# Decay logits of a gated linear attention from one rounded product with 98 rows, and eight dense products per tile at another place

## What is computed

```python
h = rmsnorm(x, norm_g)
proj = h @ w_in       # q, k, v of three branches, low-rank decay features glr, z paths, gates
gate_logits = einsum('btir,irk->btik', glr, w2) + b2      # glr: 2 directions x rank 16; k: 4 heads x 64
log_a = log_sigmoid(gate_logits) / 16                     # the decays of both directions
o_a = gla_branch(q, k, v, log_a) * silu(z_a)              # chunked scan, forward and backward
o_b = diff_attention(...) * silu(z_b)
o_c = memory_cross_attention(...) * silu(z_c)
x = x + (sum_i sigmoid(gate_i) * (o_i @ w_branch[i])) @ w_out
return rmsnorm(x, final_norm_g)
```

## Time and profile before

| what | before |
|---|---|
| median of three runs | 3404.91 us (3400.65 to 3405.81) |
| the profiled execution, its own time | 3406.49 us |
| its span, first to last instruction | 3404.7 us |
| TensorE busy | 3281.1 us, 96% of the span |
| VectorE busy | 1989.6 us, 58% |
| ScalarE busy | 1324.1 us, 39% |
| GpSimd busy | 1106.1 us, 32% |
| granted TensorE clock, mean | 0.985 |

### The profile page before, as it was taken

The page is one execution under the profiler, slowest core; times in us unless marked ns, Lnnn a source line. Parts: engine busy times, 40 slices in busy tenths (PEclk is TensorE's granted clock), DMA queues, the critical chain, the costliest instruction groups (busy, mean ns, idle before and its releaser), DMA issues. The chain is left out here.

```text
span 3404.7 us, 50932 instructions
## 1 busy us (share of the span) xinstructions
PE 3281.1 (96%) x19032; PEld 2557.6 (75%) x19032; DVE 1989.6 (58%) x4609; ACT 1324.1 (39%) x2165; POOL 1106.1 (32%) x511
## 2 busy tenths in 40 slices
PE   7999999998999999999999988999999888999998
PEld 6888888886878888888877765666666556888887
DVE  3322312226566656665568788888888566556654
ACT  3111111114334343344323336767676555333322
POOL 3322323243333343333333325555555433000000
PEclk9999999999999999999999999999999999999999
DMA  6545445565454544544448965122221266667562
GB/s 214 182 153 188 154 156 176 173 208 177 133 182 146 180 151 125 190 145 141 131 161 292 324 210 155 45 75 64 67 62 38 100 229 229 226 230 237 176 217 75
DMA packets 317906, 554.89 MB, mean 163 GB/s; under 512 B 35421, under 2 KB 114525, under 8 KB 317662
## 3 DMA queue, kind: packets, MB, share of 16 engines
q1 hardware_dynamic: 266510, 471.26, 42.9%
q10 hardware_dynamic: 51152, 80.38, 6.5%
HBM read 382.03 MB, written 169.50 MB: 162 GB/s over the span
## 5 line engine op out<-in xcount | busy, mean ns | idle before, releaser
L731 POOL TENSOR_TENSOR glaf_w_lo<-early_raw,glaf_w_hi 128x1024 fp32r<-128x1024 f32 x140 | 350.0, 2500 | 638.6 <-ACT glaf_w_hi L705 638.6
L760 PE MATMUL glaf_dense_acc<-h_hi,glaf_w_hi 128*128 128x512 f32 x1120 | 444.0, 396 | 4.1 <-ACT glaf_dense_out L714 4.1
L760 PE MATMUL glaf_dense_acc<-h_lo,glaf_w_hi 128*128 128x512 f32 x1120 | 446.6, 399 | 0.0
L760 PE MATMUL glaf_dense_acc<-h_hi,glaf_w_lo 128*128 128x512 f32 x1120 | 437.0, 391 | 0.0
L1749 DVE CUSTOM_DVE_ANT_0 front_p<-diff_s_ps,ahead_table 128x512 f32<-128x512 f32 x544 | 347.4, 687 | 74.0 <-PE diff_s_ps L1611 73.0
L514 POOL TENSOR_TENSOR proj_w_lo<-early_raw,proj_w_hi 128x1024 fp32r<-128x1024 f32 x84 | 204.6, 2438 | 478.9 <-DVE proj_w_hi L476 478.9
L1692 ACT ACTIVATE front_p<-front_p,diff_neg_max 128x2048 f32<-128x2048 f32 (+1 forms) x160 | 278.7, 1743 | 7.0 <-DVE diff_neg_max L1757 7.0
L1635 PE MATMUL diff_oT_ps<-diff_aT,diff_v 128*128 128x512 f32 x544 | 273.3, 603 | 5.2 <-ACT diff_aT L1686 5.2
L201 PE MATMUL proj_acc<-h_hi,proj_w_hi 128*128 128x512 f32 x672 | 262.8, 391 | 0.0
L203 PE MATMUL proj_acc<-h_hi,proj_w_lo 128*128 128x512 f32 x672 | 261.6, 389 | 0.0
L202 PE MATMUL proj_acc<-h_lo,proj_w_hi 128*128 128x512 f32 x672 | 261.5, 389 | 0.0
(11 more groups left out here) (215 smaller groups left out, 7149.1 us busy)
## 6 DMA issues: line engine op xcount, KB each, us to landing
early_raw<-in_w_zg SPq DMA_DIRECT2D x180, 512.0 KB, 4.7
early_raw<-in_w_stream SPq DMA_DIRECT2D x80, 512.0 KB, 3.6
scratch_zg<-glaf_dense_out SPq DMA_DIRECT2D x140, 256.0 KB, 2.3
items_raw<-in_w_br SPq DMA_DIRECT2D x120, 256.0 KB, 2.9
merge_gate<-scratch_zg SPq DMA_DIRECT2D x120, 256.0 KB, 3.2
scratch_featT<-proj_out ACTq DMA_DIRECT2D x80, 256.0 KB, 2.2
items_br_hi<-scratch_item_hi SPq DMA_DIRECT2D x60, 256.0 KB, 5.8
items_br_lo<-scratch_item_lo SPq DMA_DIRECT2D x60, 256.0 KB, 6.7
```

Source lines behind the costliest of these rows:

```text
L731: pool.tensor_tensor(self.w_lo[:, s], self.raw[:, u % self.RAW], self.w_hi[:, s], ALU.subtract).then_inc(self.lo_split, 1)
L760: done = pe.matmul(self.acc[:, u % self.banks], a, x, start=i == 0, stop=i == self.PER - 1)
```

## The change

The decay features are split in the projection. ScalarE copies rows 32 to 63 of the narrow bank to SBUF, VectorE adds them to rows 0 to 31 in PSUM, ScalarE writes the sum rounded, and VectorE writes what the rounding left. Three stores put them into `narrowT`, now 96 rows: rounded, rounded again, rest. The weights and the bias of the logits are split by four VectorE steps in the projection (`split_decay`), so that the 98 rows are high features times high weights, high times low, low times high, and two rows of ones with high and low bias. In the forward phase the logits are then one fp32r product instead of a float32 one. `SHARES` puts 30 instead of 22 dense products in front of the second level group of direction 0 and 6 instead of 14 at the tile's end. The clearing of semaphores moves from the end of the differential attention to the end of the backward phase.

```diff
+GATE_ROWS = 6 * RANK + 2
...
-        self.glr = m.sb("glr", [4 * RANK + 1, 2, P])
-        self.decay_w = m.sb("decay_w", [4 * RANK + 1, 2 * H * GK])
+        self.glr = m.sb("glr", [GATE_ROWS, 2, P], FP32R)
+        self.decay_w = m.sb("decay_w", [GATE_ROWS, 2 * H * GK], FP32R)
...
-    def load_gates(self, sp, narrowT, w2):
-        sp.dma_start(self.decay_w[:, :], w2).then_inc(self.decay_in, 16)
+    def load_decay(self, sp, raw, pick, w2, w2_pick):
+        sp.dma_start(raw, w2).then_inc(self.decay_in, 16)
+        sp.dma_start(pick, w2_pick).then_inc(self.decay_in, 16)
+
+    def split_decay(self, dve, raw, pick):
+        whole = self.decay_w[:, :].bitcast(FP32)
+        step = Chain(dve, self.decay_steps)
+        dve.wait_ge(self.decay_in, 32)
+        step(dve.tensor_copy(self.decay_w[:, :], raw))
+        step(dve.tensor_tensor(raw, raw, whole, ALU.subtract))
+        step(dve.tensor_scalar(raw, raw, pick[:, 1:2], None, ALU.mult))
+        step(dve.scalar_tensor_tensor(self.decay_w[:, :], whole, pick[:, 0:1], raw, ALU.mult, ALU.add))
+
+    def load_gates(self, sp, narrowT):
         for j in range(2):
...
+            early.load_decay(sp, decay_raw[:, :], decay_pick[:, :], w2, w2_pick)
             for c in range(NC):
                 for s in range(STREAM):
...
                 act.wait_ge(unit_done, u + 1)
                 if u >= OUTS:
                     act.wait_ge(stored[u % OUTS], 16 * (u // OUTS))
+                    if u - OUTS in narrow_units:
+                        act.wait_ge(gate_stored, 32 * (c + 1))
...
+                elif kind == "narrow":
+                    act.activation(out[0:NR, u % OUTS], acc[NR:2 * NR, u % BANKS], ACT.Copy).then_inc(gate_steps, 1)
+                    act.wait_ge(gate_steps, 3 * c + 2)
+                    act.activation(out[0:NR, u % OUTS].bitcast(FP32R), acc[0:NR, u % BANKS], ACT.Copy).then_inc(evacuated, 1)
...
                 if kind == "narrow":
-                    dst = narrowT[:, cols]
-                elif kind == "values":
+                    act.dma_start(narrowT[0:NR, cols], out[0:NR, u % OUTS]).then_inc(gate_stored, 16)
+                    act.dma_start(narrowT[NR:2 * NR, cols], out[0:NR, u % OUTS]).then_inc(gate_stored, 16)
+                    act.wait_ge(gate_steps, 3 * c + 3)
+                    act.dma_start(narrowT[2 * NR:3 * NR, cols], out[NR:2 * NR, u % OUTS]).then_inc(stored[u % OUTS], 16)
+                    return
...
+            def gate_parts(u):
+                c, s = units[u][1], u % OUTS
+                near = acc[0:NR, u % BANKS]
+                dve.wait_ge(gate_steps, 3 * c + 1)
+                dve.tensor_tensor(near, near, out[0:NR, s], ALU.add).then_inc(gate_steps, 1)
+                dve.wait_ge(evacuated, u + 1)
+                dve.tensor_tensor(out[NR:2 * NR, s], near, out[0:NR, s], ALU.subtract).then_inc(gate_steps, 1)
...
             for u, (kind, c, i, t) in enumerate(units):
                 at = u - first_unit[c]
+                if u - 1 in narrow_units:
+                    gate_parts(u - 1)
+                if u == first_unit[1]:
+                    early.split_decay(dve, decay_raw[:, :], decay_pick[:, :])
                 for n in split_at.get(u, ()):
                     split(n)
...
+                    if u - BANKS in narrow_units:
+                        pe.wait_ge(gate_steps, 3 * units[u - BANKS][1] + 3)
...
-        SHARES = [10] * X_SLOTS + [18, 22, 18, 18, 18, 14]
+        SHARES = [10] * X_SLOTS + [18, 30, 18, 18, 18, 6]
...
-                sp.dma_start(glr[0:KR - 1, j % S], narrowT[0:KR - 1, j * P:(j + 1) * P]).then_inc(glr_in[j % S], 16)
+                sp.dma_start(glr[0:KR - 2, j % S].bitcast(FP32), narrowT[:, j * P:(j + 1) * P]).then_inc(glr_in[j % S], 16)
...
-            pe.wait_ge(decay_in, 16)
+            pe.wait_ge(early.decay_steps, 4)
...
-        block = m.block(used)
+        block = m.block(used, last=True)
...
-        block = m.block(used, last=True)
+        block = m.block(used)
...
-        for part in range(2):
+        for part in range(3):
             w2[(2 * part + d) * RANK:(2 * part + d + 1) * RANK, d] = gla_gate_w2[0, d]
-        w2[4 * RANK, d] = gla_gate_b[0, d]
+        w2[6 * RANK:, d] = gla_gate_b[0, d]
+    high = np.repeat([1, 0, 1, 1, 0], [2 * RANK, 2 * RANK, 2 * RANK, 1, 1]).astype(np.float32)
```

More of the change, by code:

```diff
@@ L105, in __init__ @@
         self.decay_in = m.sem("decay_in")
+        self.decay_steps = m.sem("decay_steps")
         self.ones_ready = m.sem("ones_ready")
@@ L203, in product3, with phase_project @@
     return pe.matmul(out, a_lo, b_hi, start=False, stop=last)
-def phase_project(nc, used, h, early, w_zg, w2, ident, x_all, gains, ident_dram, w_stream, w_narrow, w_values, w_mem, w_mem_values, hT_hi, hT_lo, featT, featT_lo, narrowT, values,
+def phase_project(nc, used, h, early, w_zg, w2, w2_pick, ident, x_all, gains, ident_dram, w_stream, w_narrow, w_values, w_mem, w_mem_values, hT_hi, hT_lo, featT, featT_lo, narrowT, values,
                   memkT, mem_v):
@@ L252, in phase_project @@
         stat = m.sb("stat", [P, 2, 4])
+        decay_raw = m.sb("decay_raw", [GATE_ROWS, 2 * H * GK])
+        decay_pick = m.sb("decay_pick", [GATE_ROWS, 2])
         acc = m.ps("acc", [P, BANKS, CH])
@@ L272, in phase_project @@
         low_stored = m.sems("low_stored", 2)
+        gate_steps, gate_stored = m.sem("gate_steps"), m.sem("gate_stored")
         stored = m.sems("stored", OUTS)
@@ L341, in _ @@
                 load_piece(n)
+            sp.wait_ge(gate_stored, 32)
             sp.wait_ge(stored[narrow_units[0] % OUTS], 16 * (narrow_units[0] // OUTS + 1))
-            early.load_gates(sp, narrowT, w2)
+            early.load_gates(sp, narrowT)
             sp.wait_ge(lo_split, len(pieces))
@@ L390, in evacuate @@
                     act.activation(out[:, u % OUTS].bitcast(FP32R), acc[:, u % BANKS], ACT.Copy, scale=scale).then_inc(evacuated, 1)
-                else:
-                    filled = slice(0, 2 * NR if kind == "narrow" else P)
-                    act.activation(out[filled, u % OUTS], acc[filled, u % BANKS], ACT.Copy).then_inc(evacuated, 1)
+                elif kind == "narrow":
+                    act.activation(out[0:NR, u % OUTS], acc[NR:2 * NR, u % BANKS], ACT.Copy).then_inc(gate_steps, 1)
+                    act.wait_ge(gate_steps, 3 * c + 2)
+                    act.activation(out[0:NR, u % OUTS].bitcast(FP32R), acc[0:NR, u % BANKS], ACT.Copy).then_inc(evacuated, 1)
+                else:
+                    act.activation(out[:, u % OUTS], acc[:, u % BANKS], ACT.Copy).then_inc(evacuated, 1)
                 if u and in_parts(u - 1):
@@ L404, in evacuate @@
                     dst = memkT[i] if c == MEMC else featT[i, :, cols]
-                act.dma_start(dst, out[0:2 * NR if kind == "narrow" else P, u % OUTS]).then_inc(stored[u % OUTS], 16)
+                act.dma_start(dst, out[:, u % OUTS]).then_inc(stored[u % OUTS], 16)
             def high_resident(n):
@@ L439, in _ @@
                 act.wait_ge(low_stored[b], 16 * (len(part_units) // 2))
+            act.wait_ge(gate_stored, 32 * NC)
             for b in range(OUTS):
@@ L790, in phase_gla_forward @@
         glr, decay_w, glr_in, decay_in = early.glr, early.decay_w, early.glr_in, early.decay_in
-        m.allocated += [*glr_in, decay_in, early.ones_ready]
+        m.allocated += [*glr_in, decay_in, early.decay_steps, early.ones_ready]
         log = m.sb("log", [P, N2])
@@ L2365, in build @@
     featT_lo = scratch("featT_lo", 2 * H, P, TOK)
-    featT, glrT = scratch("featT", N_FEAT, P, TOK), scratch("glrT", 4 * RANK, TOK)
+    featT, glrT = scratch("featT", N_FEAT, P, TOK), scratch("glrT", 6 * RANK, TOK)
     memkT, mem_v = scratch("memkT", H, P, MEM), scratch("mem_v", MEM, W)
@@ L2383, in build @@
                 early = Early(nc, gla_ctx)
-                phase_project(nc, used, h, early, w_zg, w2, ident_tile, x_all, gains, ident, w_stream, w_glr, w_values, w_mem, w_mem_values, hT_hi, hT_lo,
+                phase_project(nc, used, h, early, w_zg, w2, w2_pick, ident_tile, x_all, gains, ident, w_stream, w_glr, w_values, w_mem, w_mem_values, hT_hi, hT_lo,
                               featT, featT_lo, glrT, [gla_v, diff_v], memkT, mem_v)
@@ L2436, in layout @@
         "w_mem_values": column_block(w_mem_kv[0], W, W),
-        "w2": w2.reshape(4 * RANK + 1, -1),
+        "w2": w2.reshape(GATE_ROWS, -1),
+        "w2_pick": np.stack([high, 1 - high], axis=1),
         "gla_sums": sums.reshape(P, 2, -1),
```

11 lines of the change are left out of this document (6 added, 5 removed).

## The result

The changed kernel took 3385.55 us, median of four runs (3380.6 to 3387.87), against 3403.4 us for the kernel before beside it: ratio 0.9945, interval 0.9933 to 0.9956. That is 18 us less. Run twice more, the same kernel gave 0.9961 (0.9946 to 0.9976) and 0.9954 (0.9941 to 0.9966). All three intervals overlap; the three medians mean 0.47%, some 16 us.

The account below looks back on a forecast made before the run. TensorE was taken as the bound, busy all of each regular forward tile. Savings of 11.7 + 0.5 + 1.7 less 0.6 us made 13.3 us off 3404.9: 3391.6 us, range 3386.5 to 3399.

Parts of the forecast that it names:

- The price of the product: Forward phase: one fp32r logits product costs 0.23 us like a dense one, saving 0.65 us each in tiles 1 to 18.
- The chain on VectorE: Regular tiles: GpSimd blocks Q, rounding becomes fast, copies end 0.3 to 0.6 us before the second level group; no wait.
- The tile's end: End of each forward tile: six dense products instead of fourteen still cover ScalarE's and VectorE's work; cost nothing.
- The projection: Chunk 0: new steps delay the weights for stream unit 1, 0.6 us lost; bounds 0 to 2 us over five chunks.
- The clearing: Semaphore clearing at a phase border: costs at most some 2.5 us, paid once before and after; net 0, bound 1 us.
- B: Regular tiles: rounding stays slow, second level group waits up to 0.9 us in some 15; 3398 to 3405 us; chance 0.11.
- C: Forward logits: the one product is no cheaper than the float32 one; 3403.8 us, no change; chance 0.05.
- D: Tile's end: ScalarE still busy, next sums' exponents and VectorE start late; slower, 3411 us at 1.6 us late; chance 0.04.
- Tiles 1 to 18: Forward phase: 11.7 us from cheaper logits plus 1.7 us from vanished copy waits in tiles 4, 8 and 12.
- the zero for tile 0: Tile 0, forward phase: cheaper logits gain 0, since TensorE next waits 4.5 us for VectorE's L1128 anyway.
- A second zero: Phases behind the forward phase: no net change, the clearing's move only shifting cost from differential attention to backward phase.
- the first logits product: Head of the forward phase, before tile 0: saves up to 0.65 us, taken as 0.5 for possibly late second-unit low weights.

Follow-up runs that it names:

- GpSimd held: GpSimd's sixth forward-phase subtraction waits for tile 0's diagonal scores: in the kernel before 3403.69 us, 0.9993; in the changed kernel with the projection's rounding moved ahead, 3386.32 us, 0.9954.

## Why the prediction was right and where it was wrong

**Right, and shown.** The price of the product: 0.64 us saved of 0.65, tiles 0.61 us shorter. The chain on VectorE: Q blocked, the rounding free, room of 0.6 us where 0.3 to 0.6 was said; the kernels with 22 and 26 products measure the same chain at 48.56 and 47.67 us a tile. The tile's end: no cost. The projection: 0.56 us of wait in chunk 0 against 0.6. The clearing: net zero in the waits (1.3 against 1.5 us) and in the times. Of the Trainium skill's rule ("SBUF — State Buffer", section "Who interferes with whom": issue order decides who blocks, the loser blocks for the whole instruction) these runs show both orders: GpSimd ahead by 0.14 us, Q 3.40 us; Q ahead by 0.15 us, Q 1.21 us and GpSimd 3.27 us. They agree. Rivals B, C and D are out: no regular tile waits for the copies, the product has one record, no tile's sums start late. A wait for the copies as B feared comes only with fewer than 30 products there, and from the blocked Q, not from a slow rounding.

**Right by luck in part.** Tiles 1 to 18: 13.3 us over the profiles against 13.4. The parts are 18 x 0.61 = 11.0 instead of 11.7, and 2.3 instead of 1.7 for the waits, which vary between executions: two misses that cancel. (Of the 20 tiles, 15 had the same length, not 16.)

**Wrong.** As far as the traces show it, the step that failed is the zero for tile 0: "being 0.65 us earlier only makes that wait longer: 0". The profiled pair shows 4.66 us there. The wait does get longer (4.5 to 5.0 us in the long case, 2.1 to 2.8 with GpSimd held), and in these cases the tile keeps its length (51.7 and 51.8, 48.6 and 48.6 us). But the sum took the wait of 4.5 us for a fixed thing of the pipeline's filling. It depends in each execution on which of two instructions starts first, and that on the clock. The profiled pair had the long case before and the short one after. Over the profiles with unheld GpSimd the kernels with the old logits gave 51.7, 51.7, 48.6, 48.6 and 48.6 us, those with the new product and the new shares 47.0, 51.8, 51.8, 47.0 and 47.0: means 49.8 and 48.9, 0.9 us apart, with 3 and 5 us between the cases. Whether the change is worth anything there isn't shown; the 47.0 us were seen only with it. Nor does a trace show the three faster runs of the first measurement, which set its median: the profiled one was the slowest of the four, 3387.87 us. The range's lower end counted the 5 us between runs, but not that such a draw can differ between the two sides of one comparison. It missed by 1 us, and the two repeated measurements, 3390.3 and 3387.4 us, lie inside it; their intervals hold the forecast ratio of 0.9961, the first one's doesn't.

A second zero failed in the pair: the phases behind the forward phase, 3.6 us less together. Its cause is open. Also mis-sized: the first logits product, 0.5 us forecast. It saves nothing: the sum feared for the low weights of the second unit, but TensorE stands still 0.46 us for the rounding of the first dense weights. The 0.2 us in the table lie within what the clock does there: the stage took 11.5 to 11.8 us in seven of the eight traces with the new product and 11.7 to 11.8 in five of the six with the old one.

**Open.** 13.3 us in the tiles and 0.9 in tile 0, less 0.9 up to the first sums (781.7 and 782.6 us, means of six traces each that lie up to 3 us apart), make some 13 us; the three medians mean 16. The profiles put the rest behind the forward phase: from the first product of the backward phase to the end the kernels with the old logits took 1651.2 us (six profiles, 1649 to 1653), those with the new ones and one clearing 1648.8 (seven, 1646 to 1649.5). The program there is the same but for the clearing's place, and the move alone made no difference in the times. Whether these 2 us are more than the luck of where TensorE runs at half clock isn't settled.

## What to carry to other kernels

When work is taken from the engine that bounds the kernel, look at what it covered: here the cheaper product alone made the kernel slower by 0.2%, and four or eight dense products at another place decided. A trace of another tile of the same kernel, one without the operation in question, priced both the saving and the new meeting of GpSimd and VectorE to 0.1 us. And before a wait of one profile enters a sum as fixed, ask whether two instructions start within some tenths of a microsecond of each other ahead of it; if so, put both cases in the range. A saving at the head of a phase is worth nothing if the next instruction then waits for another engine: look at what it needs.

## What was not expected of the hardware

Two executions of one program differed by 4.8 us in one 47 us tile. In the traces of tile 0 a GpSimd subtraction and a VectorE multiplication start 0.01 to 0.6 us apart, in one or the other order. Where GpSimd was first, VectorE's step took 3.35 us instead of 1.21; where VectorE was first by 0.15 us, it took 1.21 and GpSimd's step 3.27 instead of 2.4. Holding GpSimd back took 3.2 us off the tile; the remaining 1.6 us lay in 30 products, a part of which TensorE made at half clock in one execution and none in the other. And clearing semaphores at a phase border cost 0.9 us for one phase's and 1.3 to 1.5 us for three or four phases'.
